# Two-layer hybrid trunk on one core: the FFN norms' sum by a streamed matmul with ones, the root over 128x256 into rB, two unread matmuls behind

## The chip, the cores and the metric

The kernel runs on one core of a Trainium2 chip. The metric is the device time of one execution in microseconds. TensorE is PE in the profile (PEld its weight loads), VectorE is DVE, ScalarE is ACT, GpSimd is POOL, SyncE is SP, whose queue starts nearly all DMAs.

## The reference, cut to what matters

The trunk has two layers. Each adds a half-step SwiGLU FFN, a mixer (sliding-window attention beside gated linear attention, behind one input projection), and a second half-step FFN; a final norm closes it. 256 tokens, width 1024, FFN width 2816, all float32.

```python
def rmsnorm(x, g):
    xf = x.astype(jnp.float32)
    y = xf * lax.rsqrt(jnp.mean(xf * xf, axis=-1, keepdims=True) + EPS)
    return (y * g.astype(jnp.float32)).astype(x.dtype)

for l in range(DEPTH):                      # DEPTH = 2
    x = x + 0.5 * swiglu(rmsnorm(x, ffn1_norm[l]), ...)
    x = x + hybrid_mixer(rmsnorm(x, mix_norm[l]), ...)
    x = x + 0.5 * swiglu(rmsnorm(x, ffn2_norm[l]), ...)
return rmsnorm(x, final_norm)
```

There are seven norms: four ahead of an FFN, two ahead of a mixer, the final one. The change is to the four.

## The kernel before, in words

**Layout.** Everything is kept transposed: 128 features on the partitions, eight such tiles (KT), the 256 tokens as columns. A norm's sum of squares therefore runs over partitions and tiles, and its result r is one number per token, that is per column, needed on all partitions.

**Matmuls.** Weights come by DMA in units of 1 MB into three slots (`raw`), ACT rounds them to a high part (`whi`), DVE subtracts for a low part (`wlo`, L1153). Each product is three one-pass matmuls over 256 columns, `three()` in L401 to L403: high times high, high times low, low times high. A unit has 48 of them in the FFNs. An FFN is 33 units: for each of its eleven groups of 256 hidden columns one gate, one up and one down unit. The gain is multiplied into x ahead of the matmuls (`xhi`, `xlo`), r only behind them: `gate_out` (L1263) and `up_out` (L1268) on DVE multiply the products by `rB`, r on all partitions (128x256). So PE starts an FFN's first units before r is known, and r has to be in `rB` when the first gate product is evacuated.

**A norm ahead of an FFN.** DVE adds the squared tiles to `sqsum` (128x256, L1234), with eps folded in. PE's `square_sums` (L481) multiplies it, 128 tokens at a time as the weights, by one column of ones: two float32 matmuls of one column, the sums of 128 tokens each on the partitions. DVE's `norm_r` waits for `ss_done` and takes the root in eight dependent instructions over 128x2 (`rsqrt`, L1218 to L1229, each waits for the one before) into `rs_y`. PE's `spread_r` waits for the last step (`rs_step`) and turns each column, broadcast, by a transpose (L489) into bank 3, columns 256 to 511. DVE's `norm_b` waits for `rb_ps` and copies that to `rB` (L1255). A norm ahead of a mixer does the same with `rcol` in the place of `rs_y`, because the column form is needed there too; the final norm has code of its own.

**Order.** Each engine runs a list of its own, written out by hand, and waits on semaphores. On PE: `begin_ffn` runs the first gate unit into bank 2 and half of the first up unit, then `square_sums`, then the other half; `ffn` goes on with half of the second gate unit, `spread_r`, the other half, the second up unit, and the first down unit, which waits for `hlo_done`. On DVE, in `ffn`: `norm_r`, the split of the next up unit (`split_lo(0)`), `norm_b`, `gate_out`, `up_out` with the product h (L1271), the split of the down unit, and h's low part (`h_lo`, L1275). The very first FFN has `first_units` in the place of this: its first three units are worked in five pieces as the DMAs land, on DVE the fourth unit is split in quarters (`fourth_lo`, L1179) around the norm, and the first down unit's weights are split in halves (`half_lo`, L1189), the first of which PE awaits at the start of its first down unit (`half_split`).

**Unread matmuls.** `half_rows` (L495) issues two float32 matmuls of 64 rows, 128x128, into a bank that nobody reads then. It stands behind the first FFN's spread, behind its first down unit, and behind the transposes in the mixer's output projection.

## Time and profile before

| | us |
|---|---|
| median of three runs | 925.46 |
| lowest, highest | 924.49, 925.49 |
| the profiled execution | 924.28 |
| its span, first to last instruction | 922.5 |

| engine | busy us | share | instructions |
|---|---|---|---|
| PE | 914.4 | 99% | 8100 |
| DVE | 606.2 | 66% | 723 |
| ACT | 455.7 | 49% | 527 |
| POOL | 3.5 | 0% | 7 |

A busy PE is not PE at its peak: a matmul's record is longer than the step to the next one, since they are pipelined, so the steps between starts are what counts. Durations of records are a matmul's latency. A float32 matmul stands as two records, each with its own weight load.

### The profile page before, as it was taken

To read this page: it belongs to the slowest core of one execution; us is meant where nothing else is said; L and a number is where in the kernel's file an instruction comes from. 1 tells how busy PE (TensorE), PEld (TensorE's weight loads), DVE (VectorE), ACT (ScalarE), POOL (GpSimd) and SP (SyncE) were. 2 spreads that over 40 slices of the span, in tenths; PEclk is the share of its full clock that TensorE was granted. 3 is DMA by queue.
4 is the path that set the end of the run, shared out by engine and by line. 5 is a ranking of instruction groups with operands and counts; after the bars stand their busy time and mean duration, and the time that the engine had idled before them with its cause. 6 is when DMAs were issued, how large, how long until landed. Compare 5 with 4: busy or idle time off the path is not lost.

```text
span 922.5 us, 19279 instructions
## 1 busy us (share of the span) xinstructions
PE 914.4 (99%) x8100; PEld 907.6 (98%) x8100; DVE 606.2 (66%) x723; ACT 455.7 (49%) x527; POOL 3.5 (0%) x7
## 2 busy tenths in 40 slices
PE   9999999999999999999999999999999999999997
PEld 9999999999999999999999999999999999999996
DVE  7755565688768665555685555567797685565554
ACT  7544443468756444444554444445685644444443
POOL 0000000000000000000000000000000000000001
PEclk9999999999999999999999999999999999999999
DMA  8765665664356655655556665665623676655631
GB/s 285 243 225 182 201 204 186 185 181 120 90 169 220 223 187 183 199 191 200 182 186 212 192 194 182 198 209 142 211 65 92 228 229 189 215 188 183 197 121 46
DMA packets 131191, 169.16 MB, mean 183 GB/s; under 512 B 3440, under 2 KB 116944, under 8 KB 131152
## 3 DMA queue, kind: packets, MB, share of 16 engines
q1 hardware_dynamic: 130576, 167.96, 57.2%
q10 hardware_dynamic: 576, 0.66, 0.2%
q8 instruction: 28, 0.46, 0.2%
q14 instruction: 11, 0.09, 0.0%
HBM read 167.55 MB, written 1.05 MB: 183 GB/s over the span
## 4 chain that ended last, share of the span: by engine, by line
PE 97%; DMA 1%; DVE 0%; SPq 0%; ACT 0%; POOL 0%; POOLq 0%; issue 0%
PE ps L401 31%; PE ps L403 30%; PE ps L402 30%; PE ps L673 1%; PE ps L660 1%; DMA resid<-in_xt 1%; PE ps L522 1%; PE ps L530 0%; PE ps L538 0%; PE ps L793 0%; PE ps L495 0%; PE ps L489 0%; PE ps L755 0%; PE ps L732 0%; PE ps L481 0%; PE ps L775 0%
## 5 line engine op out<-in xcount | busy, mean ns | idle before, releaser
L1153 DVE TENSOR_TENSOR wlo<-raw,whi 128x2048 fp32r<-128x2048 f32 x157 | 351.2, 2238 | 234.2 <-ACT whi L880 234.1
L401 PE MATMUL ps<-xhi,whi 128*128 128x256 f32 x1584 | 438.7, 277 | 0.0
L402 PE MATMUL ps<-xlo,whi 128*128 128x256 f32 x1584 | 437.3, 276 | 0.0
L403 PE MATMUL ps<-xhi,wlo 128*128 128x256 f32 x1584 | 437.3, 276 | 0.0
L880 ACT ACTIVATE whi<-raw 128x2048 fp32r<-128x2048 f32 x157 | 294.1, 1873 | 129.1 <-PE ps L403 128.6
L401 PEld LDWEIGHTS ps<-xhi,whi 128*128 128x128 f32 x1584 | 297.4, 188 | 0.6
L403 PEld LDWEIGHTS ps<-xhi,wlo 128*128 128x128 f32 x1584 | 297.4, 188 | 0.0
L402 PEld LDWEIGHTS ps<-xlo,whi 128*128 128x128 f32 x1584 | 297.4, 188 | 0.0
L401 PE MATMUL ps<-h_parts,whi 128*128 128x256 f32 x768 | 212.3, 276 | 0.0
L402 PE MATMUL ps<-h_parts,whi 128*128 128x256 f32 x768 | 212.2, 276 | 0.0
L403 PE MATMUL ps<-h_parts,wlo 128*128 128x256 f32 x768 | 212.1, 276 | 0.0
L401 PEld LDWEIGHTS ps<-h_parts,whi 128*128 128x128 f32 x768 | 144.3, 188 | 0.2
L402 PEld LDWEIGHTS ps<-h_parts,whi 128*128 128x128 f32 x768 | 144.2, 188 | 0.0
L403 PEld LDWEIGHTS ps<-h_parts,wlo 128*128 128x128 f32 x768 | 144.2, 188 | 0.0
L930 ACT ACTIVATE h_parts<-work 128x512 fp32r<-128x512 f32 x44 | 27.8, 633 | 144.5 <-DVE work L1271 144.5
L923 ACT ACTIVATE work<-work 128x512 f32<-128x512 f32 x44 | 27.8, 632 | 128.0 <-DVE work L1263 128.0
L1275 DVE TENSOR_TENSOR h_parts<-work,h_parts 128x512 fp32r<-128x512 f32 x44 | 30.4, 692 | 31.8 <-ACT h_parts L930 31.7
L401 PE MATMUL ps<-whi,xhi 128*128 128x256 f32 (+1 forms) x128 | 36.6, 286 | 0.0
L403 PE MATMUL ps<-whi,xlo 128*128 128x256 f32 (+1 forms) x128 | 35.9, 280 | 0.0
L402 PE MATMUL ps<-wlo,xhi 128*128 128x256 f32 (+1 forms) x128 | 35.8, 280 | 0.0
L1271 DVE TENSOR_TENSOR work<-work 128x512 f32<-128x512 f32 x44 | 30.5, 692 | 1.9 <-ACT work L923 0.5
L1268 DVE TENSOR_TENSOR work<-ps,rB 128x512 f32<-128x512 f32 x44 | 30.1, 684 | 2.1 <-PE ps L403 2.1
(173 smaller groups left out, 544.4 us busy)
## 6 DMA issues: line engine op xcount, KB each, us to landing
raw<-in_ffn_w_down SPq DMA_DIRECT2D x44, 1024.0 KB, 4.9
raw<-in_ffn_w_gate SPq DMA_DIRECT2D x42, 1024.0 KB, 5.4
raw<-in_ffn_w_up SPq DMA_DIRECT2D x42, 1024.0 KB, 5.4
raw<-in_w_in SPq DMA_DIRECT2D x12, 1024.0 KB, 5.2
raw<-in_w_in SPq DMA_DIRECT2D x8, 512.0 KB, 4.5
raw<-in_w_out SPq DMA_DIRECT2D x8, 512.0 KB, 4.7
raw<-in_w_in SPq DMA_DIRECT2D x2, 1088.0 KB, 5.2
raw<-in_w_out SPq DMA_DIRECT2D x8, 256.0 KB, 3.7
```

What stands on the lines that cost most here:

```text
L401: pe.matmul(o, w_hi, x_hi, start=start, stop=False, skip_group_check=True)
L402: pe.matmul(o, w_hi, x_lo, start=False, stop=False, skip_group_check=True)
L403: return pe.matmul(o, w_lo, x_hi, start=False, stop=stop, skip_group_check=True)
L522: pe.matmul(tiles(bank)[:, ft, :], weights(u, k, UC, ft * P, P)[0], xhi[:, k, :], start=k == 0 and ft == 0, stop=False, skip_group_check=True)
L660: last = pe.matmul(ps[bank][:, a:a + n], qT[b:b + HD, j, t * P:(t + 1) * P], kv[b:b + HD, 0, last_key - n:last_key], start=True, stop=True ...
L880: nc.scalar.activation(h, r, ACT.Copy).then_inc(hi_done, 1)
L923: nc.scalar.activation(s32[:, :, :], a32[:, :, :], ACT.Silu).then_inc(silu_done, 1)
L930: nc.scalar.activation(hhi[hb][:, :, :], h32[:, :, :], ACT.Copy).then_inc(hhi_done, 1)
L1153: nc.vector.tensor_tensor(lo, r, h.bitcast(F32), ALU.subtract).then_inc(lo_done, 1)
L1268: nc.vector.tensor_tensor(u32[:, :, :], tiles(bank), r_tiles(2), ALU.mult).then_inc(u_done, 1)
L1271: nc.vector.tensor_tensor(h32[:, :, :], s32[:, :, :], u32[:, :, :], ALU.mult).then_inc(h_done, 1)
L1275: nc.vector.tensor_tensor(hlo[hb][:, :, :], h32[:, :, :], hhi[hb][:, :, :].bitcast(F32), ALU.subtract).then_inc(hlo_done, 1)
```

## The change

For the four norms ahead of an FFN, the weights are the 128x128 ones, and `sqsum` is streamed through them in one float32 matmul of 256 columns (`sums_everywhere`); the sum of each token lands on all partitions, in bank 3, columns 256 to 511. `norm_everywhere` takes the root there, over 128x256, straight into `rB`, with `work[:, 6]` as the second buffer, and raises `rb_done` itself. The spread by transposes and the copy to `rB` go for these four. In `begin_ffn` two unread matmuls of 64 rows (`half_rows`) follow the sum; in the first FFN the two that stood behind the spread stay where they were. The mixer norms and the final norm keep their form, with `rb_ps` counted anew.

```diff
--- before.py
+++ after.py
@@ -482,6 +482,12 @@
                                      start=True, stop=True, skip_group_check=True)
                 last.then_inc(ss_done, 1)
 
+            def sums_everywhere(v):
+
+                pe.wait_ge(sqsum_done, v + 1)
+                pe.matmul(ps[3][:, 256:512], ones[:, :], sqsum[:, :],
+                          start=True, stop=True, skip_group_check=True).then_inc(ss_done, 1)
+
             def spread(o, call, y, n):
 
                 pe.wait_ge(rs_step, RS * (call + 1))
@@ -550,14 +556,13 @@
                         piece_hi(1, p, 7)
                     piece_lo(0, p, 2)
                     if p == LAST:
-                        square_sums(0)
+                        sums_everywhere(0)
                     if p >= 2:
                         piece_hi(1, p, 7)
                     piece_hi(2, p, 0)
                     piece_lo(1, p, 7)
                     if p == LAST:
                         pe.wait_ge(s_cst, 16)
-                        spread_r(0, rs_y)
                         half_rows(5)
                     piece_lo(2, p, 0)
 
@@ -581,7 +586,8 @@
 
                 pe.wait_ge(resid_up, 4 * (v + 1))
                 up_tile(tiles(7)[:, 0, :], 1, 0)
-                square_sums(v)
+                sums_everywhere(v)
+                half_rows(1)
                 up_tile(tiles(7)[:, 1, :], 1, 1).then_inc(unit_done, 1)
 
             def ffn(f, l):
@@ -594,7 +600,6 @@
                 else:
                     split_ready(2, t)
                     up_tile(tiles(0)[:, 0, :], 2, 0)
-                    spread_r(5 * l + 4 * f, rs_y)
                     up_tile(tiles(0)[:, 1, :], 2, 1).then_inc(unit_done, 1)
                     up(0, t + 1, 1)
                 pe.wait_ge(hlo_done, grp + 1)
@@ -1136,7 +1141,7 @@
                 nc.scalar.activation(sq[:, some, :], resid[:, some, :], ACT.Square).then_inc(sq_done, 1)
                 for m in ((0, 1), (2, 3), (), (4,), (5, 6, 7))[n]:
                     scaled(m)
-            act.wait_ge(rb_ps, v + 2)
+            act.wait_ge(rb_ps, DEPTH + 2)
             nc.scalar.copy(rB[:, :], ps[0][:, 0:256]).then_inc(r_copied, 1)
             for n in (2, 4):
                 a, b = ENDS[n]
@@ -1205,9 +1210,9 @@
                 gain_lo(v, KT - 2, gain)
                 gain_lo(v, KT - 1, gain)
 
-            def rsqrt(call, s, n, count, y):
-
-                base, a = RS * call, rs_a[:, 0:n]
+            def rsqrt(call, s, n, count, y, a=None):
+
+                base, a = RS * call, rs_a[:, 0:n] if a is None else a
                 scale = 0.375 * count ** 0.5
 
                 def then(k, ins):
@@ -1250,8 +1255,15 @@
                 dve.wait_ge(sum_step, steps + 2)
                 add_eps(sqsum[:, :], sq[:, 0, :], sq[:, 1, :], D).then_inc(sqsum_done, 1)
 
-            def norm_b(v):
-                dve.wait_ge(rb_ps, v + 1)
+            def norm_everywhere(v, call):
+
+                dve.wait_ge(ss_done, v + 1)
+                rsqrt(call, ps[3][:, 256:512], SEQ, D, rB[:, :], a=work[:, 6, :])
+                dve.wait_ge(rs_step, RS * (call + 1))
+                dve.sem_inc(rb_done, 1)
+
+            def norm_b(l):
+                dve.wait_ge(rb_ps, l + 1)
                 nc.vector.tensor_copy(rB[:, :], ps[3][:, 256:512]).then_inc(rb_done, 1)
 
             def r_tiles(n):
@@ -1290,9 +1302,8 @@
                 t = l * TURNS + FFN_TURN[f]
                 grp = (2 * l + f) * GROUPS
                 if l or f:
-                    norm_r(v, 5 * l + 4 * f, rs_y)
+                    norm_everywhere(v, 5 * l + 4 * f)
                     split_lo(0, t + 1)
-                    norm_b(v)
                     dve.wait_ge(rb_done, v + 1)
                     gate_out(grp, 3 * t, 2)
                     up_out(grp, 3 * t + 1, 7)
@@ -1300,9 +1311,8 @@
                     h_lo(0, grp)
                 else:
                     fourth_lo(0)
-                    norm_r(0, 0, rs_y)
+                    norm_everywhere(0, 0)
                     fourth_lo(1)
-                    norm_b(0)
                     dve.wait_ge(rb_done, 1)
                     gate_out(0, 0, 2)
                     fourth_lo(2)
@@ -1345,7 +1355,7 @@
                 split_mix(2)
                 norm_r(v, 5 * l + 1, rcol)
                 split_mix(3)
-                norm_b(v)
+                norm_b(l)
                 dve.wait_ge(lr_tok_ev, 2 * ev)
                 for n in (0, 2):
                     nc.vector.tensor_copy(lr_tok[:, :, n * STEP:n * STEP + RANK].bitcast(F32R), lr32[:, :, :]).then_inc(lr_hi, 1)
@@ -1590,7 +1600,7 @@
             last_residual(7, 8, 2)
             dve.wait_ge(ss_done, v + 1)
             rsqrt(5 * DEPTH, ps[3][:, 0:TT], TT, D, rs_y[:, 0:TT])
-            dve.wait_ge(rb_ps, v + 1)
+            dve.wait_ge(rb_ps, DEPTH + 1)
             dve.wait_ge(scaled_done, KT)
             for n, (a, b) in enumerate(ENDS[:-1]):
                 nc.vector.tensor_tensor(sq[:, a:b, :], work[:, a:b, :],
```

## Rows read from the trace of the kernel before

**Rows 1.** The page, busy time, share of the span and instructions of each engine.

```profile
PE 914.4 (99%) x8100; PEld 907.6 (98%) x8100; DVE 606.2 (66%) x723; ACT 455.7 (49%) x527; POOL 3.5 (0%) x7
```

**Rows 2.** The page, the chain that ended last, by engine.

```profile
PE 97%; DMA 1%; DVE 0%; SPq 0%; ACT 0%; POOL 0%; POOLq 0%; issue 0%
```

**Rows 3.** The waits of PE: engine, line, releaser: us, times, longest.

```profile
PE ps L489 <- DVE rs_y L1229: 0.5, 1, 0.5
```

**Rows 4.** Windows: stretch, its us, busy us (instructions) by engine, granted clock, DMA, GB/s.

```profile
257.00:262.00 5.00, 5.00 (x44) 5.00 (x44) 4.02 (x9) 3.71 (x4) 0.00 (x0) 1.00 0.00 0
...
300.00:400.00 100.00, 100.00 (x885) 100.00 (x884) 59.48 (x45) 41.18 (x31) 0.00 (x0) 1.00 0.62 199
```

**Rows 5.** The timeline (start, us), PE, around the column sums of layer 0's second FFN.

```profile
288.57 0.28 PE L403 MATMUL ps<-xhi,wlo 128*128 128x256 f32 x1
288.68 0.55 PE L481 MATMUL ps<-ones,sqsum 128*128 128x1 f32 x4
...
289.88 0.28 PE L401 MATMUL ps<-xhi,whi 128*128 128x256 f32 x1
```

**Rows 6.** The timeline, PE, around the spread of the same FFN.

```profile
294.52 0.28 PE L403 MATMUL ps<-xhi,wlo 128*128 128x256 f32 x1
294.64 0.38 PE L489 MATMUL ps<-cst,rs_y 128*128 128x128 f32 x2
...
295.45 0.28 PE L403 MATMUL ps<-xhi,wlo 128*128 128x256 f32 x1
```

**Rows 7.** The timeline, PE, around unread matmuls that stand between two streams.

```profile
36.03 0.28 PE L403 MATMUL ps<-h_parts,wlo 128*128 128x256 f32 x1
36.23 0.71 PE L495 MATMUL ps<-cst 64*128 64x128 f32 x4
...
37.22 0.28 PE L403 MATMUL ps<-xhi,wlo 128*128 128x256 f32 x1
```

**Rows 8.** Float32 matmuls of more columns: timeline of L829, groups by form of L660.

```profile
262.48 1.04 PE L829 MATMUL ps<-cst,work 128*128 128x128 f32 x8
...
L660 PE MATMUL ps<-kv,qT 64*128 64x192 f32 x32 | 4.8, 361 | 0.0
...
L660 PE MATMUL ps<-kv,qT 64*128 64x128 f32 x32 | 3.5, 270 | 0.0
```

**Rows 9.** The timeline, PE, first FFN: column sums, spread, unread matmuls.

```profile
20.95 0.50 PE L481 MATMUL ps<-ones,sqsum 128*128 128x1 f32 x4
...
23.29 0.38 PE L489 MATMUL ps<-cst,rs_y 128*128 128x128 f32 x2
23.60 0.71 PE L495 MATMUL ps<-cst 64*128 64x128 f32 x4
```

**Rows 10.** The timeline, DVE, first FFN: root, quarter split, copy, gate product, half split.

```profile
21.50 0.16 DVE L1218 TENSOR_SCALAR rs_y<-ps 128x2 int32<-128x2 int32 x1 [0.41 <-PE ps L481]
...
22.85 0.16 DVE L1229 SCALAR_TENSOR_TENSOR rs_y<-rs_a,rs_y 128x2 f32<-128x2 f32 x1
22.93 0.68 DVE L1179 TENSOR_TENSOR wlo<-raw,whi 128x512 fp32r<-128x512 f32 x1
23.71 0.42 DVE L1255 COPY rB<-ps 128x256 f32<-128x256 f32 x1
24.17 0.69 DVE L1263 TENSOR_TENSOR work<-ps,rB 128x512 f32<-128x512 f32 x1
...
28.09 1.22 DVE L1189 TENSOR_TENSOR wlo<-raw,whi 128x1024 fp32r<-128x1024 f32 x1
```

**Rows 11.** Line 1234: duration in ns, minimum, median, maximum; first and last start.

```profile
L1234 DVE SCALAR_TENSOR_TENSOR sqsum<-sq x6: 424/426/426, 20.0 to 739.9; 128x256 f32<-128x256 f32 x6
```

**Rows 12.** The timeline, DVE, layer 0's second FFN: the copy, h's low part.

```profile
295.05 0.42 DVE L1255 COPY rB<-ps 128x256 f32<-128x256 f32 x1 [0.65 <-PE ps L489]
...
299.78 0.69 DVE L1275 TENSOR_TENSOR h_parts<-work,h_parts 128x512 fp32r<-128x512 f32 x1
```

**Rows 13.** The timeline, weight loads: first FFN's first down unit; the column sums.

```profile
30.59 0.19 PEld L401 LDWEIGHTS ps<-h_parts,whi 128*128 128x128 f32 x1
...
288.62 0.19 PEld L481 LDWEIGHTS ps<-ones,sqsum 128*128 128x128 f32 x1
```

## Prediction, made before the changed kernel was run

> **What bounds the kernel now.** I read the page first: PE is busy for 914.4 of 922.5 us, DVE and ACT for two thirds and a half of it [rows 1], and the chain of work that ended last is PE for 97% [rows 2]. The list of waits says the same from the other side: of the code that is edited here only the spread behind the root waited for anybody, once, for 0.5 us, and that was in the final norm, which stays [rows 3]. So TensorE is the bound in every stage that the change touches, and it is never short of input there. Two things follow. Whatever the change adds to or takes from PE's own queue is worth its full time. Whatever it does to DVE is worth nothing as long as DVE is done before PE asks.
>
> The second thing to see is that the stream of matmuls has two paces. Per matmul of 256 columns it takes 5.00 / 42.4 = 0.118 us in one stretch and 100 / 882 = 0.1134 us in the other; the counts in the rows also hold the two or three matmuls that hang over an edge, so I took the paces from the steps between starts: 0.1134 in rows 5 to 7, and the window rows bound them [rows 4]. The granted clock is 1.00 in both. 4.4 ns is little, but an FFN is 33 units of 48 matmuls, so a whole FFN at the slower pace would cost 1584 x 4.4 ns = 7.0 us. The change must not only be costed by its own instructions but also by the pace that it leaves behind.
>
> **The change, part by part, on PE.** All costs are taken as extra time against a stream that would go on at 0.1134 us a step.
>
> Removed, column sums: from the last matmul before them (288.57) to the seventh behind them (289.88) are 1.31 us; seven steps would be 0.79. They cost 0.52 us, of which 0.05 is a wait for sqsum that stays: their first weight load starts 0.05 behind the last matmul's start, where in the stream it starts with it [rows 5, 13]. In the other two FFNs of this kind the same count gives 0.02 us less.
>
> Removed, spread: from 294.52 to 295.45 are six steps, 0.93 against 0.68: 0.25 us [rows 6].
>
> Added, two unread matmuls: the trace has the same helper between two such streams. From 36.03 to 37.22 are three steps and the helper, 1.19 against 0.34: 0.85 us [rows 7]. It is not the four short records that are dear (0.11 us each), but the two changes between 128 and 64 rows: the step from the last full matmul to the first of 64 rows is 0.20 instead of 0.11 us, and so is the one back, with 0.11 more before the second full one.
>
> Added, the sum on all partitions: a float32 matmul, ones as weights, 256 columns streamed. A float32 matmul shows as two records. The trace has none with 128 rows and 256 columns, so it is bounded. Below: two records at the pace of the kernel's one-pass matmuls, 2 x 0.113 = 0.23 us. Above: the records of 128 columns follow each other at (1.04 - 0.27) / 7 = 0.110 us, and from 128 to 192 columns a record grows by 361 - 270 = 91 ns, which for 128 more columns is 0.18; 2 x (0.11 + 0.18) = 0.58 us [rows 8]. I take 2 x 0.216 = 0.43: 0.110 us for 128 columns is two cycles of 2.4 GHz for each and 3 ns, where the 256 columns of the big stream need one each (107 of 113 ns), and the 361 is a mean with first records of a group in it. With the 0.05 of the wait the sum adds 0.48 us ahead of the two unread matmuls.
>
> TensorE: Matmul & The Clock Gate of the Trainium skill, section Back-to-back issue gap, gives 262 cycles for 256 columns and does not tell element types apart; as an estimate by that, one 0.11 us piece would do, and the whole change would come out 0.32 x 4 = 1.3 us cheaper than by my rows. The rows speak against it: 128 float32 columns already take 0.110 us, twice over.
>
> Net at each of the three FFNs that begin behind another stage (after the mixer of either layer, and into layer 1): 0.48 + 0.85 - 0.52 - 0.25 = +0.56, with the 0.02 of the other two +0.58. Three times: **+1.73 us**.
>
> The first FFN differs, since its two unread matmuls are there already. The column sums go (0.37 us from 20.95 to 21.32) and two records of 0.216 come: +0.07. The spread goes with its two records of 0.11, and the full matmul in front of it now pays the step to 64 rows that the second transpose paid (23.29 to 23.60 is 0.31, the step itself 0.20): -0.22 [rows 9]. Net **-0.15 us**.
>
> **On DVE.** The root is eight dependent instructions. Over 128x2 they take 22.85 - 21.50 = 1.35 us for seven steps, 0.193 each, of which 0.16 is the instruction and 0.033 the hand-over [rows 10]. Over 128x256 no such chain is there; scalar_tensor_tensor of that shape takes 0.426 us [rows 11], the copy from PSUM of that shape 0.42 [rows 10]. Below: half of it for the one single-input instruction, if it ran at double rate. Above: 0.46 a step. I take 0.426 + 0.033 = 0.459, eight of them 3.67 against 1.54. The copy of rB falls away, 0.46 with its hand-over, and in the first FFN 0.17 of waiting for the transposes (the quarter split in front of it starts at 22.93, the next instruction could start 0.61 later, as behind the other splits of that size, but the copy starts at 23.71). What stands behind the root moves by 3.67 - 1.54 - 0.46 - 0.17 + 0.08 (the float32 sum ends later than the column sums did) = **1.6 us** in the first FFN.
>
> VectorE: DVE Perf Modes of the Trainium skill, section on the TRN2 errata, has one formula with a fixed part of 58 cycles and another with 151. As an estimate, 256 elements take 0.327 us by the first and 0.424 by the second. The row agrees with the second; the first would make the chain 2.9 us and is the page's side of the first rival below.
>
> Who waits for it. In the three later FFNs, nobody: behind the root stands the split of the next up weights. It was over 0.65 us ahead of 295.05, at 294.4 [rows 12]; with the root 2.1 us longer it ends at 296.5, and PE asks for it 19 matmuls behind 295.45, at 297.6 [rows 6], and later still by the 0.56 above. DVE loses its wait of 0.65 us for the spread and the copy [rows 12], so all behind them comes 1.0 us later: h's low part is ready at 299.78 + 0.69 + 1.0 = 301.5, while PE comes to the first down unit 48 matmuls behind 297.6, at 303.0. ACT's silu and h_hi move along inside that, and the buffer reload that waits for the split is issued 2.1 us later, and the buffer isn't read until a round of units later. In the first FFN it is tight. Behind the root stand the quarter splits of the fourth unit, the gate and up products, h, and then the split of the first half of the down weights. The split of the last quarter would end at 29.0, PE asks at 29.1: just held. The half split ends at 29.3 now [rows 10], at 30.9 then. PE asks for it with the weight load at 30.59 [rows 13], less the 0.15 it has won: 30.44. The half split is 0.5 us late, so PE stalls: **+0.50 us**. Bounds: nothing, if a step of the root takes 0.39 or less; 0.8, if a step takes 0.46 and the last quarter is late too. The time lost isn't won back, since PE has no idle time further on.
>
> **The sum.** 1.73 - 0.15 + 0.50 = +2.1 us. The profiled execution took 924.28 us with its span of 922.5, the other three 924.49, 925.46 and 925.49. On its own time the sum gives 926.4; on the median of the three 927.6; on the mean of all four, 924.9, it gives 927.0. I take 927.3, between the last two.
>
> **Rivals.**
> 1. *The cover in the first FFN holds.* One mechanism: the eight wide DVE steps take 0.39 us or less each, then the half split is ready at 30.4 and PE never stalls. Time: +1.6 us, 926.8, inside 0.2% (1.85 us), which is about what a measurement of this kernel can tell from no change; so this is the case that ends on the other side of my forecast, not slower. For it: a single-input instruction may be quicker than my row. Against: every row of 256 elements on DVE is 0.42.
> 2. *The streamed sum costs one short pass.* At 2 x 0.113 the four sums are 0.8 us cheaper, and DVE gets its sum 0.2 us earlier, which takes as much off the stall. +1.1 us, 926.3, within 0.2%. Against: the records of 128 columns.
> 3. *The pace.* A whole FFN falls to 0.118 us a matmul behind the streamed sum and the two unread matmuls do not mend it: +7.0 us for each FFN, 934.3 for one and 955 for all. For it: the stream goes into the slower pace elsewhere without any stall in sight. Against: behind the helper, and behind every other change of rows, the stream is at 0.1134 [rows 7].
> 4. *More of DVE's lateness gets through,* in all four FFNs, by the reload of buffers: +3 to +4 us, 928.5. Against: the margins above.
> 5. *Faster.* Only if the two unread matmuls cost next to nothing beside the sum, as work in rows that the array has free: 3 x (0.48 - 0.52 - 0.25) = -0.87, and -0.15 and +0.50 for the first FFN, -0.5 us. That is 924.7 and still within 0.2%; for more than that I see no path but an error of the account.
>
> TensorEngine Tiling (Array Packing) of the Trainium skill, section Key Properties, says that a change of tiling mode drains the engine. By that rule, the fifth case has no ground, and the trace agrees with 0.20 us where a step is 0.11.
>
> **How the numbers follow.** The forecast itself has 0.52, rival one 0.17, rival two 0.08, rival three 0.10, rival four 0.08, the fifth 0.05. The range reaches from 926.0 (rival two, on the lower of the runs of before) to 929.3 (forecast with the upper bounds of sum and stall, and rival four): it leaves out rival three and the fifth. The forecast lies only 0.25 us beyond 0.2%, so of its 0.52 I count 0.13 as within. Slower: 0.39 + 0.10 + 0.08 = 0.57. Within: 0.13 + 0.17 + 0.08 + 0.02 = 0.40. Faster: 0.03.
>
> **What would show it.** In the timeline of PE at the later FFNs: two records of the sum 0.216 us apart, then 0.3 to the first of four 64-row records, then the stream at 0.1134 within four steps. On DVE eight steps of 0.46. In PE's waits a new one of about 0.5 us in the first down unit, for DVE's half split, and none elsewhere. The windows over the long FFN stretches must still show 885 matmuls in 100 us; 848 would be rival three. I am wrong if that wait is missing, if the sum's records are 0.11 apart, or if the account of the two unread matmuls is not 0.85.

## The result, and the profile after

| us | before | changed |
|---|---|---|
| median of 21 runs | 924.8 | 927.74 |
| lowest, highest | 923.94, 937.99 | 926.52, 947.71 |
| the profiled execution | 924.28 | 947.44 |
| its span | 922.5 | 945.7 |

The ratio is 1.0051, with a 95% interval from 1.0036 to 1.0067: half a per cent slower. One thing must be said for any of the numbers here to be understood: executions of these kernels lie on a ladder with steps of about 6.7 us. Of the 21 runs of the changed kernel 11 lie at 926.52 to 927.74 (median 927.2), four at 932.9 to 933.5, four at 940.0 to 941.2 and two at 947.4 to 947.7; of the 21 of the kernel before, 20 lie at 923.94 to 925.49 and one at 937.99, two steps up. The ratio leaves out runs more than 1.5% above the lowest, that is five of the six on the two upper rungs (939.99 stays in) and the 937.99 of the kernel before; over all 21 runs the means are 932.8 and 925.4. On the lowest rung the change costs 2.4 us; the rest of its cost is how often it stands on a higher one. The profiled execution stands on the third step, by luck, since so it shows what a step is.

The page of the changed kernel, busy time by engine, to be laid beside [rows 1]:

```profile
PE 936.3 (99%) x8096; PEld 927.6 (98%) x8096; DVE 613.2 (65%) x719; ACT 456.8 (48%) x527; POOL 3.5 (0%) x7
```

PE has four matmul records fewer and is 22 us longer busy. Its own waits are no reason. From the waits of the changed kernel (engine, line, releaser: us in total, times, longest), those that the edit touches:

```profile
PE ps L488 <- DVE sqsum L1239: 0.8, 1, 0.8
PE ps L495 <- DVE rs_y L1234: 0.5, 1, 0.5
PE ps L401 <- DVE wlo L1194: 0.4, 1, 0.4
```

The first is one wait of 0.75 us in front of the very first sum, which waits for x to arrive and differs from execution to execution (0.30 and 0.21 in two kernels below); the later sums' waits of 0.05 us, shorter than the overlap of two records, don't show in this view. The second is the final norm's spread, as in [rows 3]; the third is the stall that I forecast, 0.38 us long. The windows tell where the 22 us are. One stretch out of the middle of each of the four FFNs, changed kernel (stretch, its us, busy us and instructions of PE, PEld, DVE, ACT, POOL, then granted clock, DMA share, GB/s):

```profile
50.00:150.00 100.00, 100.00 (x852) 100.00 (x851) 55.67 (x41) 41.01 (x30) 0.00 (x0) 1.00 0.60 194
310.00:410.00 100.00, 100.00 (x852) 100.00 (x851) 56.19 (x42) 41.09 (x30) 0.00 (x0) 1.00 0.61 191
500.00:600.00 100.00, 100.00 (x885) 100.00 (x884) 57.39 (x43) 43.34 (x32) 0.00 (x0) 1.00 0.61 200
770.00:870.00 100.00, 100.00 (x851) 100.00 (x850) 56.09 (x42) 41.19 (x30) 0.00 (x0) 1.00 0.60 191
```

The kernel before has 885 matmuls in each of these four stretches, as in [rows 4]. Here three FFNs of four have 852 or 851: one matmul every 0.1178 us where it was 0.1133. From here on these two are called the slow and the fast pace. PE is 100% busy, the granted clock is 1.00 and DVE and ACT do the same work in both. The slow pace begins in three places and nothing in the FFN ends it, the two unread matmuls behind the first down unit (37.93 us) included. It runs from 32.1 us in the first FFN, from 297.8 in layer 0's second and from 757.7 in layer 1's second. The three slow stretches have some 4556 matmuls, at 4.5 ns more each 20.5 us; with the 2.4 that is 22.9 of the 23.2 us by which this execution is longer than the one profiled before. A third of 20.5 is 6.8: the steps of the ladder are FFNs at the slower pace.

The place where the pace is decided, PE's timeline of the changed kernel around the sum (start us, duration), first in layer 0's second FFN and then in layer 1's first:

```profile
296.43 0.28 PE L403 MATMUL ps<-xhi,wlo 128*128 128x256 f32 x1
296.55 0.64 PE L488 MATMUL ps<-sqsum,ones 128*128 128x256 f32 x2
297.12 0.71 PE L501 MATMUL ps<-cst 64*128 64x128 f32 x4
297.76 0.39 PE L401 MATMUL ps<-xhi,whi 128*128 128x256 f32 x1
...
484.30 0.28 PE L403 MATMUL ps<-xhi,wlo 128*128 128x256 f32 x1
484.42 0.59 PE L488 MATMUL ps<-sqsum,ones 128*128 128x256 f32 x2
484.94 0.71 PE L501 MATMUL ps<-cst 64*128 64x128 f32 x4
485.58 0.39 PE L401 MATMUL ps<-xhi,whi 128*128 128x256 f32 x1
```

and the weight loads of the same two places:

```profile
296.32 0.19 PEld L403 LDWEIGHTS ps<-xhi,wlo 128*128 128x128 f32 x1
296.49 0.30 PEld L488 LDWEIGHTS ps<-sqsum,ones 128*128 128x128 f32 x2
...
484.19 0.19 PEld L403 LDWEIGHTS ps<-xhi,wlo 128*128 128x128 f32 x1
484.31 0.30 PEld L488 LDWEIGHTS ps<-sqsum,ones 128*128 128x128 f32 x2
```

At 484 the sum's weight load starts 0.12 us behind the one before it, as in the stream; DVE's sum had been ready. At 296 it starts 0.17 behind, because PE waits 0.05 us for `sqsum`: the wait that I had priced at 0.05 us and left at that. From 296.55 to 297.12 are 0.57 us, from 484.42 to 484.94 are 0.52. Behind the first the stream is slow and behind the second it is fast. The two places differ in one thing more, the pace at which PE comes: fast at 296, slow at 484, where it comes late because the FFN directly before had been slow. Which of the two differences counts, the experiments have to show. Either way the FFN that directly follows a slow one starts without the wait here and was fast, which fits that none of the 21 runs lies four steps up.

### The profile page after: what moved, and what is told of

Read it like the earlier page. It is cut to its first block, busy times and chain, and to the rows that moved or that the text cites. A ratio compares the mean times of both kernels' runs of the same rounds, so it can differ in the third digit from the quotient of the medians.

```text
span 945.7 us, 19270 instructions
## 1 busy us (share of the span) xinstructions
PE 936.3 (99%) x8096; PEld 927.6 (98%) x8096; DVE 613.2 (65%) x719; ACT 456.8 (48%) x527; POOL 3.5 (0%) x7
## 4 chain that ended last, share of the span: by engine, by line
PE 95%; DVE 1%; SPq 1%; DMA 1%; issue 0%; ACT 0%; POOL 0%; POOLq 0%; DVEq 0%
PE ps L401 31%; PE ps L402 30%; PE ps L403 30%; DMA raw<-in_ffn_w_gate 1%; PE ps L678 1%; SPq L277 1%; PE ps L665 1%; PE ps L501 0%; PE ps L798 0%; PE ps L760 0%; SPq L314 0%; PE ps L737 0%; PE ps L488 0%; PE ps L780 0%; PE ps L806 0%
## 5 line engine op out<-in xcount | busy, mean ns | idle before, releaser
L401 PE MATMUL ps<-xhi,whi 128*128 128x256 f32 x1584 | 443.5, 280 | 0.0
L402 PE MATMUL ps<-xlo,whi 128*128 128x256 f32 x1584 | 442.2, 279 | 0.0
L403 PE MATMUL ps<-xhi,wlo 128*128 128x256 f32 x1584 | 442.2, 279 | 0.0
L401 PE MATMUL ps<-h_parts,whi 128*128 128x256 f32 x768 | 215.1, 280 | 0.4 <-DVE wlo L1194 0.4
L402 PE MATMUL ps<-h_parts,whi 128*128 128x256 f32 x768 | 214.8, 280 | 0.0
L403 PE MATMUL ps<-h_parts,wlo 128*128 128x256 f32 x768 | 214.8, 280 | 0.0
```

Of the source, the lines that this page charges most:

```text
L401: pe.matmul(o, w_hi, x_hi, start=start, stop=False, skip_group_check=True)
L402: pe.matmul(o, w_hi, x_lo, start=False, stop=False, skip_group_check=True)
L403: return pe.matmul(o, w_lo, x_hi, start=False, stop=stop, skip_group_check=True)
```

## Experiments

All times are those of the one core used. The experiments ran in three sessions, each on a chip of its own, with runs of the kernel before beside them. In the order of the sessions: 17 (six at 923.65 to 924.75, nine near 931, two near 938.6), 23 (fourteen at 923.43 to 925.52, eight near 931.3, one of 1313.39) and 23 (sixteen at 923.5 to 925.6, one of 930.5, six at 937.7 to 939.1). So the kernel before climbs the ladder too, and in these sessions far more often than beside the first result. An odd sequence, in what follows, is whatever stands inside a stream of one-pass matmuls of 256 columns and isn't one of them. I therefore judge each experiment by its rungs and by the windows of its own profile, and give the ratio for completeness.

### The two parts alone

The sum on all partitions without the two unread matmuls:

```diff
 sums_everywhere(v)
-half_rows(1)
```

> The changed kernel without the two unread matmuls behind the streamed sum in the three later FFNs; the first FFN is that of the changed kernel. Theory 1 (the two changes between 128 and 64 rows around the unread matmuls throw the dice for the pace of the whole FFN behind them): the slower pace is gone from the three later FFNs, and the runs lie at about 924.8 us (927.1 less 3 x 0.77), with at most one step of 6.8 us from the first FFN in some of them. Theory 2 (the streamed float32 sum throws the stream into the slower pace, and the unread matmuls mend it most of the time): all or nearly all three later FFNs run at 0.118 us a matmul, and the runs lie at 945 us or more. Theory 3 (only DVE's lateness in the first FFN does it): runs at 924.8 and 931.6, never above.

Measured: 6 runs, 937.08 to 951.67, ratio 1.0146 (1.0093 to 1.0199). None is on the lowest rung or the first step. The profile (of the run at 951.67) has 851 matmuls in all four stretches. Beside it the two unread matmuls alone, in the kernel before:

```diff
 square_sums(v)
+half_rows(1)
```

> The kernel before, with two unread matmuls added behind the column sums in the three later FFNs, nothing else. Theory 1: lowest runs at 924.8 + 3 x 0.85 = 927.4 us, and others higher by one to three steps of 6.8 us, in about half of the runs. Theories 2 and 3: 927.4 us in all runs, none higher.

Measured: 12 runs: two at 926.7 to 927.0, six at 933.3 to 934.5, four at 939.3 to 940.8; ratio 1.0066 (1.003 to 1.0102). So the two unread matmuls aren't what brings the slow pace into the changed kernel: without them the streamed sum is worse. In the profile of the run at 927.03 the stream behind two of the three sums went slow all the same, for the 47 matmuls up to the spread, and the spread mended it. Two windows of this kernel, the stretch ahead of the spread and one behind it:

```profile
290.50:295.50 5.00, 5.00 (x45) 5.00 (x44) 3.79 (x10) 1.92 (x1) 0.00 (x0) 1.00 0.63 205
297.00:302.00 5.00, 5.00 (x47) 5.00 (x46) 4.83 (x6) 3.08 (x3) 0.00 (x0) 1.00 0.47 162
```

A window also counts the two or three matmuls that hang over its edges: 5.00 / 0.1178 + 2.5 is 44.9, 5.00 / 0.1134 + 2.5 is 46.6. So it is slow ahead of the spread and fast behind it. The change also takes away that spread, which could mend a slow stream here (it doesn't everywhere, as the kernels below show). Its runs one and two steps up were not profiled.

### The same instructions where PE waits for nothing

Each FFN loops over nine groups of units behind its first two, the last FFN over eight: 35 places in all. There, in front of the group's down unit, inside the stream and where PE waits for nothing, I put the unread matmuls alone (three calls' worth), and then a streamed float32 sum, of a tile nobody reads the product of, with the same matmuls behind it:

```diff
+half_rows(3)
 down(1, t + g, 0, False, alone)
```

> The kernel before, with two unread matmuls ahead of each down unit of the FFN loops (35 places), to see how often the stream behind them runs at which pace. Their own cost is 35 x 0.85 = 29.8 us. Theory 1: of the 35 stretches of 144 matmuls a share of a quarter to a half runs at 0.118 us, the others at 0.1134; 960 to 966 us. Theories 2 and 3: all 35 stretches at 0.1134 us; 954.6 us.

```diff
+pe.matmul(ps[3][:, 256:512], ones[:, :], keep[:, :], start=True, stop=True, skip_group_check=True)
+half_rows(3)
 down(1, t + g, 0, False, alone)
```

> The kernel before, with a float32 matmul of ones by 256 columns of a constant, not read, and two unread matmuls ahead of each down unit of the FFN loops (35 places). Their own cost is 35 x (0.43 + 0.10 + 0.85) = 48 us. Theory 1: the same share at the slower pace as with the two unread matmuls alone. Theory 2: clearly more than with the unread matmuls alone, where it is none. Theory 3: none in either.

Measured: 960.72 and 971.53 us, one run each, with extra work that nobody reads. The time says little, the 35 places say more. Alone, the unread matmuls left the pace as they found it: at 27 places the stream was fast before and after. In the last FFN the column sums, with their wait, had thrown it to the slow pace at 764 us, and at all 8 places there it was slow before and after, as in this stretch behind the first of them ((113 - 2.5) x 0.1178 = 13.0):

```profile
800.00:813.00 13.00, 13.00 (x113) 13.00 (x112) 7.09 (x6) 4.66 (x4) 0.00 (x0) 1.00 0.46 161
```

With the streamed sum ahead of them it was fast behind all 35, two of them in a stream that the waiting column sums had thrown to the slow pace. Windows of the second kernel, ahead of such a place (331.75 us) and behind it:

```profile
310.00:330.00 20.00, 20.00 (x173) 20.00 (x172) 13.04 (x10) 8.37 (x6) 0.00 (x0) 1.00 0.62 212
334.00:349.00 15.00, 15.00 (x134) 15.00 (x134) 9.36 (x7) 4.37 (x4) 0.00 (x0) 1.00 0.50 167
```

(173 - 2.5) x 0.1178 = 20.1 and (134 - 2.5) x 0.1134 = 14.9. So the changed kernel's own sequence, where PE doesn't wait for it, mends a slow stream. What remained was the wait.

These two profiles also hold six of the kernel before's own column sums, at their own place, each with its wait of 0.05 us and each entered at the fast pace. Behind three the stream stayed fast, behind three (at 299.94 and 776.20 us in the second kernel, 763.67 in the first) it was slow, and the spread didn't mend it. The same code with the same wait goes either way.

### Moving the sequence away from the wait

The sum and the unread matmuls go six matmuls later, into the second half of the up unit, so that `sqsum` is long ready. The same six matmuls later for the column sums of the kernel before:

```diff
-up_tile(tiles(7)[:, 0, :], 1, 0)
-sums_everywhere(v)
-half_rows(1)
-up_tile(tiles(7)[:, 1, :], 1, 1).then_inc(unit_done, 1)
+for ft in range(FT):
+    for k in range(KT):
+        w_hi, w_lo = weights(1, k, UC, ft * P, P)
+        last = three(...)
+        if ft == 1 and k == 1:
+            sums_everywhere(v)
+            half_rows(1)
+last.then_inc(unit_done, 1)
```

> The changed kernel with the streamed sum and its two unread matmuls moved behind the first six matmuls of the second half of the up unit, so that sqsum (which came 0.05 us too late) is there 0.6 us ahead. Theory W (PE's 0.05 us wait on sqsum in front of the sum leaves the pace behind it to chance; without the wait the sum and the unread matmuls always end in the faster pace): the three later FFNs run at 0.1134 in every run; times lie at 927.0 us, or one step of 6.8 us higher where the first FFN, which keeps its stall, falls into the slower pace; never two steps. Theory D (chance lies in the two changes of rows, wait or not): one to three steps in as many runs as the changed kernel, and two or more steps in some.

> The kernel before with its column sums moved by the same six matmuls, nothing else. Theory W: the wait of 0.05 us is gone and with it nearly all of the runs of before that lie 6.8 or 13.7 us above the others; all at 924.7 us (0.15 us lower for the waits). Theory D: as before on the same chip, with its own share of higher runs.

Measured for the changed kernel: 12 runs, eight at 926.55 to 928.82, four at 932.4 to 934.0, none higher; ratio 1.003 (0.9999 to 1.0061). Measured for the kernel before: 6 runs, all at 944.48 to 945.23, three steps up; ratio 1.0194 (1.0154 to 1.0235). The first is what the theory of the wait wants. The second is a miss by three steps, since I had forecast 924.7. It taught more than the hits: PE's timeline of that kernel shows no wait at the sums, they stand one step of 0.12 behind the matmul before them, and the stream is slow behind them in each of the three FFNs and in every run:

```profile
289.34 0.28 PE L403 MATMUL ps<-xhi,wlo 128*128 128x256 f32 x1
289.46 0.50 PE L481 MATMUL ps<-ones,sqsum 128*128 128x1 f32 x4
289.82 0.36 PE L401 MATMUL ps<-xhi,whi 128*128 128x256 f32 x1
```

its window in layer 0's second FFN:

```profile
310.00:410.00 100.00, 100.00 (x851) 100.00 (x850) 55.73 (x41) 41.09 (x30) 0.00 (x0) 1.00 0.59 188
```

So the theory had to be put in another way: without a wait the pace behind the odd instructions is the same in every run and hangs on what they are; with a wait in front it is open. The rest of the kernels test that. The other way about, the whole sequence earlier, so that the wait is long (about 1.07 us, twice):

```diff
-        if ft == 1 and k == 1:
+        if ft == 0 and k == 4:
```

> The changed kernel with the sum and the unread matmuls nine matmuls earlier, so that PE waits 1.07 instead of 0.05 us for sqsum in each of the three later FFNs. The waits cost 3 x 1.0 us: lowest at 930.1 us. Theory W: steps of 6.8 us as often as in the changed kernel or more. If only a wait that ends within one matmul's time does it, no steps from these three. Theory D: as in the changed kernel.

Measured: 4 runs, 936.52, 944.04, 949.89 and 950.09; ratio 1.0181 (1.0108 to 1.0254). In its profile the FFNs behind the two waits of 1.07 us are slow, the one with 0.73 us, which PE entered slow, is fast. The lowest run is one step above the 930.1 that the waits alone would give. A longer wait doesn't reset the pace: behind a long one, too, the four runs end on three different rungs.

### Which sequences give which pace

Four kernels, each with its sums at the later place, and in the three with the streamed sum the first FFN's norm as in the kernel before (there only: column sums, root over 128x2, spread and copy), so that its stall is gone:

```diff
 # changed_later, first FFN
-sums_everywhere(0)
+square_sums(0)
 ...
+spread_r(0, rs_y)
 half_rows(5)
 ...
-norm_everywhere(0, 0)
+norm_r(0, 0, rs_y)
 fourth_lo(1)
+norm_b(0)
```

> As the changed kernel with the sum moved, and the first FFN's norm as before (column sums, root over 128x2, spread). Theory W: no run above the lowest by a step; all at 926.3 us (before plus 3 x 0.56 less 3 x 0.05). If the first FFN's stall of 0.4 us had nothing to do with the slower pace there, single steps remain in some runs. Theory D: steps of 6.8 us in half of the runs.

> The changed kernel with the sum moved behind six more matmuls (no wait) and the first FFN's norm as before, without the two unread matmuls. Without a wait the pace behind a given sequence should be the same in every run. If the streamed sum by itself leaves the slower pace: three FFNs at 0.118, 944 to 945 us in every run, as the kernel before with its column sums moved. If it leaves the faster one: 923.7 us in every run (925.9 less 3 x 0.77), under the kernel before.

> The same with one unread matmul of 64 rows behind the sum instead of two. If the change of rows does the mending, one is enough: 925.3 us in every run (925.9 less 3 x 0.22). If it takes the number of records that two have: 944 us.

The second has no `half_rows(1)`, the third one unread matmul in its place:

```diff
-half_rows(1)
+pe.matmul(ps[1][:, 0:P], ident[0:HD, :], ident[0:HD, :], start=True, stop=True, skip_group_check=True)
```

and the fourth is the kernel before with `square_sums(v)` moved and `half_rows(1)` behind it:

> The kernel before with its column sums moved (which alone gave the slower pace in all three later FFNs, 944.9 us in every run) and two unread matmuls behind them. If the unread matmuls mend what stands in front of them whenever PE doesn't wait: 927.4 us in every run. If only the streamed float32 sum together with them does: 947 us in every run, or in between, since the spread that follows can mend too.

| the three later FFNs, no wait in front | runs | us | steps up | ratio |
|---|---|---|---|---|
| streamed sum, two unread | 12 | 925.49 to 927.97, median 925.95 | 0 | 0.9994 (0.9969 to 1.0019) |
| streamed sum, none | 4 | 943.97 to 945.07 | 3 | 1.022 (1.0204 to 1.0237) |
| streamed sum, one unread | 10 | 924.93 to 926.75, median 925.54 | 0 | 1.0014 (1.0005 to 1.0024) |
| column sums, none | 6 | 944.48 to 945.23 | 3 | 1.0194 (1.0154 to 1.0235) |
| column sums, two unread | 10 | 925.68 to 927.14, median 926.37 | 0 | 1.0017 (1.0001 to 1.0032) |

42 runs, and each kernel keeps to one rung. Before the runs I had left it open between 925.3 and 944 us for the streamed sum with one unread matmul, and between 927.4 and 947 for the column sums with two. The windows of the second FFN of layer 0, streamed sum with none (first) and with one unread matmul:

```profile
310.00:410.00 100.00, 100.00 (x851) 100.00 (x851) 56.59 (x43) 41.38 (x30) 0.00 (x0) 1.00 0.58 189
```

```profile
310.00:410.00 100.00, 100.00 (x885) 100.00 (x884) 59.08 (x46) 42.84 (x32) 0.00 (x0) 1.00 0.61 194
```

### The counter-test: the wait stays, the first FFN's stall goes

The changed kernel with only its first FFN's norm as before, so that the wait of 0.05 us stays in front of the three later sums:

> The changed kernel with only the first FFN's norm put back to that of before; the sum stands where the change put it, with its wait of 0.05 us in the three later FFNs. If the wait is what leaves the pace to chance: lowest runs at 926.4 us, and steps of 6.8 us in several runs, up to three in one; with the sum moved there were none in 12 runs.

Measured: 6 runs, 932.55 and five at 939.23 to 939.98; ratio 1.0153 (1.0124 to 1.0183). The profile, of a run at 939.5:

```profile
288.42 0.28 PE L403 MATMUL ps<-xhi,wlo 128*128 128x256 f32 x1
288.53 0.64 PE L488 MATMUL ps<-sqsum,ones 128*128 128x256 f32 x2
...
476.29 0.28 PE L403 MATMUL ps<-xhi,wlo 128*128 128x256 f32 x1
476.40 0.59 PE L488 MATMUL ps<-sqsum,ones 128*128 128x256 f32 x2
```

Its windows over the same four stretches:

```profile
50.00:150.00 100.00, 100.00 (x884) 100.00 (x884) 58.87 (x44) 41.07 (x30) 0.00 (x0) 1.00 0.59 194
310.00:410.00 100.00, 100.00 (x852) 100.00 (x851) 55.72 (x41) 41.41 (x30) 0.00 (x0) 1.00 0.59 189
500.00:600.00 100.00, 100.00 (x885) 100.00 (x884) 59.08 (x43) 41.53 (x31) 0.00 (x0) 1.00 0.60 194
770.00:870.00 100.00, 100.00 (x852) 100.00 (x851) 55.72 (x42) 41.41 (x30) 0.00 (x0) 1.00 0.58 189
```

A record pair of 0.64 with the wait and a slow FFN behind it; a pair of 0.59 without the wait, since PE came late out of the slow FFN, and a fast one behind it; then the wait and the slow pace again. The twin whose sums stand six matmuls later has 12 runs and its highest is 927.97. Its profile also says which of the two differences between 296 and 484 us counted in the changed kernel: PE enters all three of its sums at the fast pace, without a wait, and leaves them fast. I had put the lowest run at 926.4; none of the six is there. Five of the six have two steps, as many as there are if every second one of three FFNs goes slow, and none has three.

Two things weaken the pair. The twins ran on different chips; but the kernel before climbed on both (8 of 22 runs, one of 1313.39 left out, and 7 of 23), and two kernels of the table with moved sums kept to the lowest rung on the chip of the counter-test (20 runs). And the move changes the place along with the wait. At the unmoved place PE comes without a wait only out of a slow FFN, three times in the profiles, and each time the pace behind is the one that the same sequence has at the later place: fast at 484.42 in the changed kernel and at 476.40 here, both with two unread matmuls, and slow behind the streamed sum alone in the changed kernel without them:

```profile
482.91 0.28 PE L403 MATMUL ps<-xhi,wlo 128*128 128x256 f32 x1
483.03 0.59 PE L488 MATMUL ps<-sqsum,ones 128*128 128x256 f32 x2
```

```profile
500.00:600.00 100.00, 100.00 (x851) 100.00 (x851) 56.77 (x42) 40.79 (x31) 0.00 (x0) 1.00 0.57 188
```

As far as these profiles reach, it is the wait and not the place that lets the slow pace in at these sums.

## Why the prediction was wrong, step by step

The median, 927.74, lies in the range from 926.0 to 929.3, and the lowest rung, +2.4 us, is close to the forecast of +2.1. But the measured change, by the ratio, is 0.51% or 4.7 us, over twice the forecast, and by the means over all runs it is 7.4 us. The sum of instructions and stalls was nearly right, and in part by luck; the term for the pace was at nothing.

**The price of the pieces was right.** With no wait, from the last matmul ahead of the sum to the seventh behind the unread ones are 1.29 to 1.30 us above seven steps of 0.1134 (the changed kernel at 484.30, and the two kernels with the sum and the two unread matmuls at the later place). I had 0.43 + 0.85 = 1.28. With the wait it is 1.34 against 1.33. The two records of the sum start 0.215 us apart, forecast 0.216; that settles that 256 float32 columns cost two of them, and rival two, which had one short pass, is out. The sum over the three later FFNs was to be +1.73. Measured with the wait gone and the first FFN as before: 925.95 against 924.6, the middle of the kernel before's own lowest rung beside it, +1.35, where my terms without the three waits of 0.05 give +1.58.

TensorE: Matmul & The Clock Gate of the Trainium skill, section Back-to-back issue gap, gives 262 cycles as the gap of a matmul of 256 columns taken by itself and does not tell element types apart. The trace does not agree for float32: two records 0.215 us apart, each with its own weight load. For the kernel's one-pass matmuls one figure isn't enough: the rows show 0.1133 and 0.1178 us for the same shape at the same granted clock.

**The DVE side was right in the step and 0.3 us off at its two ends.** DVE's timeline of the changed kernel in the first FFN, to be laid beside [rows 10]:

```profile
22.43 0.42 DVE L1223 TENSOR_SCALAR rB<-ps 128x256 int32<-128x256 int32 x1 [0.19 <-PE ps L488]
22.89 0.42 DVE L1224 TENSOR_TENSOR work<-rB 128x256 f32<-128x256 f32 x1
...
25.63 0.42 DVE L1234 SCALAR_TENSOR_TENSOR rB<-work,rB 128x256 f32<-128x256 f32 x1
26.22 0.69 DVE L1184 TENSOR_TENSOR wlo<-raw,whi 128x512 fp32r<-128x512 f32 x1 [0.16 <-DVE rB L1234]
```

Eight steps of 0.459, as forecast. But `norm_everywhere` ends with a wait for its own last step and an increment of `rb_done`, and the next instruction starts 0.16 us after the root's end, where I had it overlap by 0.08 as independent DVE instructions do in [rows 10]: 0.24 us. The root itself starts 0.74 us behind the start of the sum (21.69), where it was 0.55 behind that of the column sums; I had 0.08 of these 0.19. The quarter split and the half split come that much later, and the last quarter, which I had "just held", isn't:

```profile
29.78 0.28 PE L403 MATMUL ps<-xhi,wlo 128*128 128x256 f32 x1
30.09 0.38 PE L401 MATMUL ps<-xhi,whi 128*128 128x256 f32 x1
...
31.45 0.28 PE L403 MATMUL ps<-xhi,wlo 128*128 128x256 f32 x1
32.11 0.36 PE L401 MATMUL ps<-h_parts,whi 128*128 128x256 f32 x1 [0.38 <-DVE wlo L1194]
```

A step of 0.31 and one of 0.66 where others are 0.11: 0.75 us more than the stream, of which the waits' row shows 0.38 in one place, against my 0.50 and within my bound of 0.8. I put the first FFN at +0.35; the pair with and without its change (lowest rungs 927.1 and 925.95) says +1.1 to +1.2, of which 0.75 - 0.15 are 0.6. The other half us isn't settled; in the profile of the kernel with the later sums the steps from 25.23 to 29.36 us are 0.118, which is 0.15 us of it. So the lowest rung stands at +2.4 where I had +2.1, with the first FFN some 0.8 dearer and the others 0.2 cheaper than I said (the lowest rung of the kernel before itself lies at 924.0 to 924.8 in the four sessions, so these don't add up to the tenth). That the errors offset each other is luck, but the hiding places and the late engine were the right ones. Of the rivals the first (the cover holds) and the fourth (lateness in all four FFNs) are out by the same rows: there is one new wait, and only in the first FFN. The fifth is out as well: two unread matmuls cost the same 0.85 beside the streamed sum as elsewhere.

**What failed is the step that let the pace alone.** The sum of the prediction takes every matmul behind the sum and the two unread ones at 0.1134 us, that is, it has the term for the pace at nothing; it counted rival three, the pace, at 0.10 and left it out of the range. The runs showed in its place an FFN at 0.1178 us a matmul for each step: 18 steps in 21 runs, 5.8 us a run on average, and at least one in 10 of the 21. Rival three had the size right, 7.0 us for an FFN against 6.7 to 6.8. Two sentences of the prediction gave it away. "Behind the helper, and behind every other change of rows, the stream is at 0.1134" rested on one profiled execution, which was one without a step, and there on places each of which has its own sequence; the loop kernel shows that unread matmuls alone keep whatever pace they find. And of the 0.05 us in front of the sums I asked what it costs, and not what it makes uncertain. The same wait stood in front of the column sums, and the six of them in the loop kernels went either way. The kernel before is on a higher rung in one of 21 runs beside the first result and in 26 of 62 in the sessions of the experiments; that this is the same wait at work is argued from those six, since no execution of it on a higher rung was profiled.

**What stays open.** Why the engine has two paces at one clock, and what a wait of 0.05 us changes inside it, no run shows; the experiments give the rule from outside, and for FFNs alone. In the mixer the pace also changes where nothing odd stands in the stream and PE doesn't wait: in the kernel before it goes from fast to slow at 256.82 us, where the stream passes from one product's operands to the next (the slow stretch of [rows 4]); in the changed kernel without the unread matmuls it goes from slow to fast at the same passage, at 264.35. That the waiting sum with two unread matmuls can also come out fast is read from the rungs: the six in the profiles that PE entered at the fast pace all came out slow. How often the waiting sequence comes out slow differs from session to session and no forecast of mine would have given it: from 1 in 21 to 11 in 17 for the kernel before. In the first FFN the slow pace began behind the stall of 0.38 us in the profiled run; that this stall lets it in is argued from one pair on one chip (with the stall 4 of 12 runs have just one step, without it 0 of 12) and from that profile. In the profile of the kernel with the later sums the same stall of 0.4 us left the stream fast. A wide root without the stall in the first FFN was not tried.

## What to carry to other kernels

Where one engine is busy all the time, its pace between the edits is the largest term: count the instructions in long windows of each stage, in more than one execution, before the few instructions that you change. Ahead of an instruction that breaks a uniform stream take out even a wait that costs next to nothing, by moving the instruction some places later than its input; here the pace behind it was then the same in every run, and one can look for the sequence that gives the good one. Here one unread matmul behind the streamed sum does, at 925.54 in the median and 926.75 at most, which doesn't beat the kernel before on its lowest rung beside it (924.4), but does in the mean of the runs beside it (925.6 against 928.3), since none of its 10 runs climbed.

## What the runs showed of the hardware

- A stream of one-pass matmuls of 128x256, each with its weight load, has two stable paces at a granted clock of 1.00: 0.1133 and 0.1178 us a matmul (885 or 852 in 100 us). It kept either through a whole FFN of 1584 matmuls.
- Inside an FFN the last odd sequence decided. Without a wait in front: streamed float32 sum with one or two 64-row matmuls, fast, out of a slow stream too; streamed sum alone or column sums alone (the spread 40 matmuls behind them), slow; column sums with two, fast; two 64-row matmuls alone, as it was before. With a wait of 0.05 us in front the same sequence came out either way (column sums in the profiles, the streamed sum by its rungs), and with one of 1.07 us too, by its rungs. In the mixer the pace also changed with no odd sequence and no wait, at 256.82 us of the kernel before.
- A wait of DVE for its own last result and an increment behind it put 0.16 us behind that result's end, where independent instructions overlap by 0.08: 0.24 us for this hand-over on the same engine. An instruction of the root starts 0.034 behind the end of the one it depends on.
- The float32 sum of 256 columns is two records 0.215 us apart. VectorE: DVE Perf Modes of the Trainium skill, section on the TRN2 errata, has a formula with a fixed part of 151 cycles that gives, as an estimate, 0.424 us for 256 elements; the eight wide steps of the root agree with 0.425.
